# A Fourier and gated mixer on one core: where the transposes of the values, a gate product and two low parts are made

## What is computed

```
def mixer_ab(h, w_in, v_g, s_w, s_b, w_out):
    z = h @ w_in
    u, v, g_a, x_b, g_b = jnp.split(z, [A_W, 2 * A_W, 3 * A_W, 3 * A_W + B_W], axis=-1)
    v = layer_norm(v, v_g).reshape(bsz, L // CHUNK, CHUNK, A_HEADS, A_HEAD_DIM)
    sv = jnp.einsum('bnphc,hqp->bnqhc', v, s_w) + s_b.T[:, :, None]
    y_a = u * sv.reshape(bsz, L, A_W) * jax.nn.silu(g_a)
    xb = x_b.reshape(bsz, L, B_GROUPS, B_GROUP_DIM).astype(jnp.float32)
    f = jnp.real(jnp.fft.fft2(xb, axes=(1, 3), norm='ortho')).astype(h.dtype).reshape(bsz, L, B_W)
    y_b = f * jax.nn.silu(g_b)
    return jnp.concatenate([y_a, y_b], axis=-1) @ w_out
```

## Time and profile before

| what | value |
|---|---|
| median of three runs | 1686.3 us (1679.79 to 1690.04) |
| the profiled execution's own time | 1682.23 us |
| its span, first to last instruction | 1680.5 us |
| TensorE busy | 1582.7 us, 94% of the span |
| VectorE busy | 1037.6 us, 62% |
| ScalarE busy | 514.7 us, 31% |
| GpSimd busy | 893.0 us, 53% |
| mean granted TensorE clock | 0.98 |

### The profile page before, as it was taken

How to read it: one execution, slowest core, us unless ns; L and a number is a source line. 1 busy time by engine, 2 the same in 40 slices (tenths; PEclk the granted TensorE clock), 3 DMA queues, 4 the chain that set the end, 5 groups by cost and what they waited for, 6 DMA issues and landing times.

```text
span 1680.5 us, 29124 instructions
## 1 busy us (share of the span) xinstructions
PE 1582.7 (94%) x10740; PEld 1369.2 (81%) x10740; DVE 1037.6 (62%) x1561; ACT 514.7 (31%) x1093; POOL 893.0 (53%) x838
## 2 busy tenths in 40 slices
PE   6999997999999999998988999999997999999997
PEld 4888865897888888988887878788995988998885
DVE  4599826469737877885767877776325666565001
ACT  4311012121146753333225555554214110111111
POOL 1455420566773408663236654434471777777774
PEclk8999999999999999999999999999998999999999
DMA  8346321323210003221111111111231232333322
GB/s 313 114 134 205 126 69 31 108 69 95 76 38 2 27 1 88 76 78 49 38 51 39 39 51 51 38 50 51 64 89 38 77 98 87 95 92 101 96 85 93
DMA packets 208568, 131.08 MB, mean 78 GB/s; under 512 B 5294, under 2 KB 194254, under 8 KB 208350
## 3 DMA queue, kind: packets, MB, share of 16 engines
q1 hardware_dynamic: 208478, 129.82, 25.9%
HBM read 127.71 MB, written 2.10 MB: 77 GB/s over the span
## 4 chain that ended last, share of the span: by engine, by line
PE 83%; DVE 10%; ACT 3%; issue 2%; DMA 1%; SPq 0%; DVEq 0%; ACTq 0%
PE ps L2264 21%; PE ps L2265 20%; PE ps L2267 20%; PE ps L2583 2%; PE ps L2609 2%; PE ps L2901 2%; DVE sb_sum L2092 1%; PE ps L2570 1%; DMA ada_first<-in_ada_w 1%; PE ps L2808 1%; PE ps L2561 1%; PE ps L2876 1%; PE ps L2712 1%; PE ps L2470 1%; PE ps L2811 1%
## 5 line engine op out<-in xcount | busy, mean ns | idle before, releaser
L749 POOL TENSOR_SCALAR w_hi<-raw 128x512 fp32r<-128x512 f32 x370 | 273.8, 740 | 682.6 <-PE ps L2267 230.8
L751 POOL TENSOR_TENSOR w_lo<-raw,w_hi 128x512 fp32r<-128x512 f32 x370 | 525.5, 1420 | 30.9
L2264 PE MATMUL ps<-xn_hi,w_hi 128*128 128x264 f32 (+1 forms) x800 | 234.9, 314 | 12.3 <-ACT xbc L1193 5.5
L2264 PE MATMUL ps<-op_hi,w_hi 128*128 128x512 f32 x608 | 215.5, 354 | 1.8 <-DVE op_lo L1489 1.7
L2265 PE MATMUL ps<-xn_lo,w_hi 128*128 128x264 f32 (+1 forms) x800 | 213.7, 287 | 0.0
L2265 PE MATMUL ps<-op_lo,w_hi 128*128 128x512 f32 x608 | 204.9, 354 | 0.0
L2267 PE MATMUL ps<-op_hi,w_lo 128*128 128x512 f32 x608 | 177.9, 352 | 0.0
L2264 PEld LDWEIGHTS ps<-xn_hi,w_hi 128*128 128x128 f32 x800 | 153.0, 191 | 26.4 <-issue 12.6
L2264 PE MATMUL ps<-u_hi,w_hi 128*128 128x258 f32 (+1 forms) x528 | 163.2, 323 | 5.7 <-DVE u_lo L2151 5.4
L2267 PE MATMUL ps<-xn_hi,w_lo 128*128 128x264 f32 (+1 forms) x800 | 164.0, 287 | 0.0
L2265 PE MATMUL ps<-u_lo,w_hi 128*128 128x258 f32 (+1 forms) x528 | 162.9, 322 | 0.0
(11 more groups left out here) (440 smaller groups left out, 3199.1 us busy)
## 6 DMA issues: line engine op xcount, KB each, us to landing
raw<-in_w_in SPq DMA_DIRECT2D x45, 512.0 KB, 3.8
raw<-in_w_up SPq DMA_DIRECT2D x44, 512.0 KB, 3.7
ada_ring<-in_ada_w SPq DMA_DIRECT2D x14, 1024.0 KB, 5.2
raw<-in_w_in_ab SPq DMA_DIRECT2D x20, 512.0 KB, 5.7
raw<-in_w_in_c SPq DMA_DIRECT2D x20, 512.0 KB, 3.7
ada_first<-in_ada_w SPq DMA_DIRECT2D x4, 2048.0 KB, 17.0
raw<-in_w_out SPq DMA_DIRECT2D x16, 512.0 KB, 3.6
raw<-in_w_down SPq DMA_DIRECT2D x16, 512.0 KB, 3.6
```

Of the source, the lines that this page charges most:

```text
L749: steps(nc.gpsimd.tensor_scalar(hi, r, 1.0, 0.0, ALU.mult, ALU.add))
L751: nc.gpsimd.tensor_tensor(lo, r, hi.bitcast(F32), ALU.subtract)\
L2264: mm(o[:, 512 * b:512 * b + n], w_h[:, k, :], hi[:, k0 + k, c0:c0 + n], start=a, stop=False)
```

## The change

It does five things, all in the mixer's stage.

1. `turn_v(t)` and `v_norm(t)` use banks 7 and 6 in turn, so `turn_v(t)` waits only for the `v_norm` two tiles back.
2. On TensorE `turn_v(2g+1)` stands ahead of `tokens(g)` in place of behind it; in the third round the transposes of the spatial weights follow it, also ahead of `tokens(2)`, and wait there for the loads of the small inputs and for the fifth `v_norm`.
3. VectorE multiplies u with silu(g_a) for all four heads at once, right behind the folding of x_b, in the projections' stage. Each head's y_a then has two operations in place of three.
4. ScalarE and VectorE make the high and low parts of chunks 4 and 5 within the second and third round; the low part of chunk 6 moves behind the first head, that of chunk h-1 stays behind head h.
5. VectorE waits for its own product of the last head before it writes `gmlp` again.

The diff:

```diff
--- before.py
+++ after.py
@@ -1042,13 +1042,8 @@
                 nc.scalar.copy(pq[g % 2][:, :, :], ps[:, 4 * 512:4 * 512 + SX].rearrange("p (t n) -> p t n", t=SX // P // 2))\
                   .then_inc(s["pq_ready"], 1)
 
-            take_pq(0)
-            for g in range(3):
-                v_std(2 * g)
-                take_pq(g + 1)
-                v_std(2 * g + 1)
-            for n, k in enumerate(Y0_ORDER):
-                if n == 0:
+            def y0_hi(k):
+                if k == 4:
 
                     act.wait_ge(s["slab_done"], SLAB0["wo_ab"])
                 if k < 4:
@@ -1056,6 +1051,16 @@
                 else:
                     act.wait_ge(s["yb_ready"], k - 3)
                 nc.scalar.copy(op_hi[:, k, :], y0_chunk(k)).then_inc(s["op_hi"], 1)
+
+            take_pq(0)
+            for g in range(3):
+                v_std(2 * g)
+                take_pq(g + 1)
+                v_std(2 * g + 1)
+                if g:
+                    y0_hi(3 + g)
+            for k in Y0_ORDER[2:]:
+                y0_hi(k)
 
             for k in range(KC):
                 b = BLOCK0["wo_ab"] + k
@@ -1607,6 +1612,9 @@
             steps(nc.vector.tensor_copy(folded[:, :, 0, 0:S // 2 + 1:S // 2], ones_of))
             steps(nc.vector.memset(folded[:, :, 1, 0:S // 2 + 1:S // 2], 0.0))
             steps.wait()
+            for h in range(4):
+                steps(nc.vector.tensor_tensor(zT[:, h, :], zT[:, h, :], zT[:, 8 + h, :], ALU.mult))
+            steps.wait()
             dve.wait_ge(s["ada_summed"], 1)
             nc.vector.tensor_copy(ada_acc[0:2 * ADA_B0, ADA_B0 - 1, 0, :], bank(7)[0:2 * ADA_B0, :]).then_inc(s["ada_taken"], 1)
             dve.wait_ge(s["ada_sums"], 1)
@@ -1622,7 +1630,7 @@
             def v_norm(t):
 
                 dve.wait_ge(s["v_turned"], t + 1)
-                v_ps = bank(7)[:, :]
+                v_ps = bank(7 - t % 2)[:, :]
                 if t:
 
                     dve.wait_ge(s["v_ready"], t)
@@ -1642,6 +1650,11 @@
                 nc.vector.scalar_tensor_tensor(zT[:, 12 + g, S:SX], f_ps[:, S:SX], float(np.sqrt(S / CTX)),
                                                zT[:, 16 + g, S:SX], ALU.mult, ALU.mult).then_inc(s["yb_ready"], 1)
 
+            def y0_lo(k):
+                dve.wait_ge(s["op_hi"], OP_DONE["l0"] + Y0_ORDER.index(k) + 1)
+                nc.vector.tensor_tensor(op_lo[:, k, :], y0_chunk(k), op_hi[:, k, :].bitcast(F32), ALU.subtract)\
+                  .then_inc(s["op_ready"], 1)
+
             for g in range(3):
                 v_norm(2 * g)
                 v_norm(2 * g + 1)
@@ -1650,29 +1663,23 @@
                     dve.wait_ge(s["sw_turned"], 1)
                     nc.vector.tensor_copy(swT[:, :, :].rearrange("p h q -> p (h q)"), bank(7)[:, :])\
                       .then_inc(s["sw_ready"], 1)
+                if g:
+                    y0_lo(3 + g)
                 fourier_gate(g)
 
-            def y0_lo(k):
-                dve.wait_ge(s["op_hi"], OP_DONE["l0"] + Y0_ORDER.index(k) + 1)
-                nc.vector.tensor_tensor(op_lo[:, k, :], y0_chunk(k), op_hi[:, k, :].bitcast(F32), ALU.subtract)\
-                  .then_inc(s["op_ready"], 1)
-
             dve.wait_ge(s["small_in"], SMALL)
-            for k in range(4, 7):
-                y0_lo(k)
             for h in range(4):
                 dve.wait_ge(s["spatial"], h + 1)
+                if h:
+                    dve.wait_ge(s["ya_ready"], h)
                 nt = SX // P
                 steps(nc.vector.scalar_tensor_tensor(
                     gmlp[:, :].rearrange("p (t q) -> p t q", t=nt),
                     pair_ps[h % 2][:, 0:SX].rearrange("p (t q) -> p t q", t=nt), col("v_norm", h),
                     s_bias[:, h:h + 1, :].to_broadcast([P, nt, P]), ALU.mult, ALU.add))
                 steps.wait()
-                steps(nc.vector.tensor_tensor(zT[:, h, :], zT[:, h, :], gmlp[:, :], ALU.mult))
-                steps.wait()
-                nc.vector.tensor_tensor(zT[:, h, :], zT[:, h, :], zT[:, 8 + h, :], ALU.mult).then_inc(s["ya_ready"], 1)
-                if h:
-                    y0_lo(h - 1)
+                nc.vector.tensor_tensor(zT[:, h, :], zT[:, h, :], gmlp[:, :], ALU.mult).then_inc(s["ya_ready"], 1)
+                y0_lo(h - 1 if h else 6)
             fourier_gate(3)
             y0_lo(3)
             y0_lo(7)
@@ -2436,11 +2443,11 @@
             pe.wait_ge(s["dft_in"], 16 * 2)
 
             def turn_v(t):
-                if t:
-
-                    pe.wait_ge(s["v_ready"], t)
+                if t >= 2:
+
+                    pe.wait_ge(s["v_ready"], t - 1)
                 for h in range(4):
-                    ins = nc.tensor.transpose(bank(7)[:, h * P:(h + 1) * P], zT[:, 4 + h, t * P:(t + 1) * P],
+                    ins = nc.tensor.transpose(bank(7 - t % 2)[:, h * P:(h + 1) * P], zT[:, 4 + h, t * P:(t + 1) * P],
                                               ident[:, :])
                 ins.then_inc(s["v_turned"], 1)
 
@@ -2477,13 +2484,15 @@
             for g in range(3):
                 turn_v(2 * g)
                 channels(g + 1)
+                turn_v(2 * g + 1)
+                if g == 2:
+                    pe.wait_ge(s["small_in"], SMALL)
+                    pe.wait_ge(s["v_ready"], SX // P - 1)
+                    for h in range(4):
+                        ins = nc.tensor.transpose(bank(7)[:, h * P:(h + 1) * P], sw[:, h, :], ident[:, :])
+                    ins.then_inc(s["sw_turned"], 1)
                 tokens(g)
-                turn_v(2 * g + 1)
-            pe.wait_ge(s["small_in"], SMALL)
             pe.wait_ge(s["v_ready"], SX // P)
-            for h in range(4):
-                ins = nc.tensor.transpose(bank(7)[:, h * P:(h + 1) * P], sw[:, h, :], ident[:, :])
-            ins.then_inc(s["sw_turned"], 1)
             pe.wait_ge(s["sw_ready"], 1)
             pe.wait_ge(s["pq_ready"], 4)
             for h in range(4):
```

## The result

The changed kernel takes 1672.58 us, median of seven runs (1667.99 to 1676.02), the kernel before beside it 1682.98 (1679.79 to 1690.04). The ratio is 0.9922, 95% interval 0.9899 to 0.9946, so 13.1 us less, between 9.1 and 17.0. A second set of runs, e11, gave 0.9913 (0.9891 to 0.9935), 14.7 us less. The medians taken alone differ by 10.4 us in the first set and by 16.0 in the second, so whole runs fix the gain to some 4 us and no better. Forecast were 1675 and 11 us.

The account below looks back on a forecast made before the run. It took TensorE's waits in the mixer's stage (14.2 of 55 us) as the bound, 12.9 us of them targeted. The walk gave 11.1 us, taken as 11 off the median of 1686.3: 1675 us, range 1665 to 1685.

Parts of the forecast that it names:

- Rounds: Mixer's stage, transforms and transposes: waits of 2.38 us go, spatial products start at 259.87 against 268.08, 8.2 us earlier.
- the new wait ahead of the weights: End of the rounds: TensorE waits 0.2 us for the fifth norm before it turns the spatial weights in bank 7.
- Heads: Spatial products of the heads: head 3 starts at 266.35 against 277.44, 11.1 us earlier, 2.9 from this part.
- To the end: From head 3 on: w_out block starts at 271.9, not 283.01; last low part 3.6 us behind, no chunk late.
- Costed at nothing: Mainly the four products of u and gate: 3.9 us of VectorE, covered by 12.33 us idle before 223.36.
- The sum: Whole kernel: 11.1 us by the walk, 10.5 by the waits, 10 to 12 as bounds; 11 taken, giving 1675.
- my rival with the clock: Mixer's stage: the clock gives something back as well, 3.4 us for one slow stretch spared, 1672 us; chance 0.05.
- The slower rival: Last two rounds: small pieces lower the clock to 0.50 until the w_out blocks; 30 us gives 1690; chance 0.04.

Follow-up runs that it names:

- e11: The changed kernel again, no further edit, in a second set of runs: stage 38.3 us, ratio 0.9913.
- e2: The kernel before with only the change's two banks and new TensorE order, gate product and low parts as before: stage 41.6 us, ratio 0.9950.
- e5: The changed kernel with TensorE's rounds in the old order, the two banks kept: stage 43.0 us, one execution.
- e1: The kernel before with only the gate product of all four heads moved ahead of the stage: stage 48.0 us, ratio 0.9991.
- e3: The changed kernel without its moved low parts, those of chunks 4, 5 and 6 ahead of the first head: stage 40.6 us, ratio 0.9926.
- e6: The changed kernel with the four gate products moved just ahead of the semaphore that starts the stage: stage 40.3 us, begun 3.6 later, ratio 0.9935.
- e7: The changed kernel with three more VectorE products in each of rounds 2 and 3: stage 41.7 us, one execution.
- e9: The kernel before, unedited, profiled a second time: stage 52.1 us, one execution.
- e10: The kernel before, unedited, profiled a third time: stage 52.2 us, one execution.

## Why the prediction held

**Rounds.** The spatial products were to start 26.6 us into the stage and start after 26.3; the new wait ahead of the weights was 0.2 and is 0.22. e2 has the same start, so this comes from banks and order alone; e5 parts them.

**Heads.** The waits for heads 0 and 1 were 0.9 and 1.3 and are 0.84 and 1.19; head 3 starts after 32.8 us for 33.1. e1, e2 and e3 give the parts at a full clock: 8.2 us from banks and order, 1.8 from the gate product and 1.5 from the low parts, 11.5 for the 11.4 measured. Of these banks and order were forecast at 7.9, the gate product at 1.9, the low parts at 1.4; the 2.3 between e3 and the change holds 0.8 of clock.

**To the end.** W_out was to start after 38.6 and starts after 38.3; the last low part comes 3.6 us behind it, the number forecast. The first matmul that reads the next attention's `pT` (L2609) is at 494.1 before and 480.6 after: 13.5 us, of which 2.3 were there at the stage's start and 11.2 are the change's. So next to nothing was given back in these 210 us. Whether all of it reaches the end the profiles cannot say, for the spans from w_out's start to the end vary by more than that: 1397.5, 1404.5 and 1404.6 us in three profiles of the old kernel, 1398.6 and 1392.7 in two of the new. The timed runs say that a gain of this size does, within their intervals.

**Costed at nothing.** The gate products are hidden, but I had their length wrong: 3.9 us, measured 5.49, since GpSimd works beside them; I had allowed GpSimd a delay and VectorE none. The 12.33 us of idle time hold both. e6 shows that the cover is what makes them free, and that without it they cost 5.5 us, not the 3.9 that I gave: 3.6 of work and 1.9 of clock.

**The sum.** The 11 us forecast are 11.4 in the pair of profiles that had the clock at 1.00. The runs show 13.1 and 14.7, with intervals that hold 11.4, so they do not show that anything was added. That the median, 1672.58, lies under 1675 is in part the base: I took three runs of the old kernel, with a median of 1686.3; with four more it is 1682.98, and 11 less is 1672.0. It is also the 1672 of my rival with the clock, so the number alone does not part the two.

What was undersized is that rival. I gave it 0.05, on the ground that the stage showed 1.00 and so the trace did not agree with what the Trainium skill says of idle gaps between bursts of matmuls (TensorE: Matmul & The Clock Gate, Why this matters for your kernels). That step failed: it rested on one execution. Two further profiles of the same kernel show the clock lowered behind the same waits, for 2.4 us, against which the change's stage is shorter by 13.8 us and not 11.4. e1, e2, e3, e5, e6 and e7, which all keep or make a wait of about 2 us or more, show it too, though in e1 and e2 it cost the stage nothing. So these profiles agree with the Trainium skill there and the first one does not. With the clock in it the forecast would have been 11 to 14 us, 1672 to 1675; how often the timed runs of the old kernel lose these 2.4 us was not observed. The slower rival had the clock wrong in sign: the rounds with their small pieces in a row kept 1.00 in all five profiles of the change and its nearest variants.

## What to carry to other kernels

Walk the dependent engines through the new order with start-to-start lengths from the trace: here it gave the changed stage to 0.3 us (38.6 for 38.3). Where TensorE waits for 2 to 4 us at once, profile several executions before you say what its clock does there: removing these waits was worth 11.4 us against one profile of the old kernel and 13.8 against two others, and adding 3.6 us to a wait cost 5.5. When work is moved into another engine's idle time, ask what GpSimd does at that time, and take the longer length.

## What the runs showed of the hardware

- The granted clock in one stretch differs between profiles of the same program: 1.00 in one, 0.72 over 18 us in two others, taken on one chip, with the same waits ahead (2.47 and 0.78 us). After a wait of 4.64 us it was 0.50 for six us (e6). Where no wait in the stage was over 1.2 us it was 1.00 in five profiles of five.
- After two waits of 2.38 us, 10 us apart, it stayed at 1.00 in all four profiles that have them (before, e1, e9, e10).
- Products of two SBUF operands on VectorE beside GpSimd's split took 1.37 us each in place of 0.89, and GpSimd's two operations 1.32 and 1.87 in place of 0.62 and 1.27.
